# The down-projection's bias moved from the experts' loop to the tail of a mixture-of-experts kernel

## The reference, cut to what matters

```python
logits = (xt @ w_router).astype(jnp.float32) + b_router
top_vals, top_idx = lax.top_k(logits, TOP_K)
gates = jax.nn.softmax(top_vals, axis=-1)
...
def expert_block(args):              # 128 tokens of one expert
    gt = xb @ w_gate[e] + b_gate[e]
    up = xb @ w_up[e] + b_up[e]
    ...
    return hdn @ w_down[e] + b_down[e]
...
y = ybuf[dest] * sg[:, None]         # times the gate of (token, expert)
h = h + (the sum of y over a token's 4 experts)
gate = jax.nn.sigmoid(rms_norm_2(h, ple_gate_norm[i]) @ w_ple_gate[i])
e = rms_norm_2(p[i] @ w_ple_proj[i], ple_post_norm[i])
h = h + gate * e
```

## Time and profile before

| what | us |
|---|---|
| median of 3 runs | 2180.78 |
| lowest and highest run | 2180.38, 2182.97 |
| the profiled execution | 2176.34 |
| its span, first to last instruction | 2174.5 |
| TensorE busy | 2102.9 (97% of the span) |
| VectorE busy | 1533.1 (71%) |
| ScalarE busy | 1379.0 (63%) |
| GpSimd busy | 254.8 (12%) |

### The profile page before, as it was taken

One profiled execution on the slowest core, in us unless ns is written; L12 is line 12 of the kernel. 1 busy time (PEld: TensorE's weight loads), 2 busy tenths in 40 slices (PEclk: granted clock), 3 DMA queues, 4 the chain that ended last, 5 costly groups with the idle time before them and its releaser, 6 DMA issues.

```text
span 2174.5 us, 31913 instructions
## 1 busy us (share of the span) xinstructions
PE 2102.9 (97%) x10614; PEld 1733.1 (80%) x10614; DVE 1533.1 (71%) x1844; ACT 1379.0 (63%) x1838; POOL 254.8 (12%) x263
## 2 busy tenths in 40 slices
PE   7997899999999998979999999999999999999999
PEld 7886778888888886768888888888888888888877
DVE  4246744232333686688989898989898989898974
ACT  3146645222323444548888888888888888888873
POOL 0000000000000000012121212212121212121210
PEclk9998999999999999989999999999999999999999
DMA  5230112222233221369999999999999999999971
GB/s 185 74 134 27 52 49 88 97 97 87 92 112 119 89 96 39 122 232 361 370 370 359 366 367 356 370 361 366 358 372 359 375 362 366 358 373 355 371 277 43
DMA packets 86560, 511.27 MB, mean 235 GB/s; under 512 B 17285, under 2 KB 18905, under 8 KB 28890
## 3 DMA queue, kind: packets, MB, share of 16 engines
q1 hardware_dynamic: 71312, 487.61, 59.8%
q0 software_dynamic: 9536, 16.81, 3.1%
q10 hardware_dynamic: 5642, 5.91, 1.0%
HBM read 503.44 MB, written 23.07 MB: 242 GB/s over the span
## 4 chain that ended last, share of the span: by engine, by line
PE 90%; DVE 4%; ACT 2%; issue 2%; DMA 1%; ACTq 0%; POOL 0%; SPq 0%; POOLq 0%; DVEq 0%
PE PS L2544 16%; PE PS L2546 16%; PE PS L2545 16%; PE PS L256 10%; PE PS L257 10%; PE PS L258 10%; PE PS L2541 2%; PE PS L2440 1%; PE PS L2554 1%; PE PS L1156 1%; PE PS L1864 1%; PE PS L1085 1%; DVE AR L1127 1%; PE PS L1801 1%; PE PS L1794 0%
## 5 line engine op out<-in xcount | busy, mean ns | idle before, releaser
L2434 DVE TENSOR_TENSOR WL<-RING,WH 128x2048 fp32r<-128x2048 f32 x385 | 873.0, 2288 | 96.1 <-ACT WH L2414 93.0
L2414 ACT ACTIVATE WH<-RING 128x1024 fp32r<-128x1024 f32 x770 | 805.9, 1059 | 181.9 <-PE PS L2546 176.3
L2544 PE MATMUL PS<-WH,RA 128*128 128x512 f32 x1540 | 640.2, 416 | 0.0
L2546 PE MATMUL PS<-WH,RA 128*128 128x512 f32 x1540 | 601.5, 391 | 0.0
L2545 PE MATMUL PS<-WL,RA 128*128 128x512 f32 x1540 | 601.0, 390 | 0.0
L2546 PEld LDWEIGHTS PS<-WH,RA 128*128 128x128 f32 x1540 | 289.8, 188 | 63.0
L2545 PEld LDWEIGHTS PS<-WL,RA 128*128 128x128 f32 x1540 | 290.6, 189 | 59.1
L2544 PEld LDWEIGHTS PS<-WH,RA 128*128 128x128 f32 x1540 | 291.6, 189 | 54.6
L256 PE MATMUL PS<-WH,RA 128*128 128x512 f32 (+2 forms) x592 | 229.5, 388 | 7.1 <-POOLq L2735 3.6
L258 PE MATMUL PS<-WH,RA 128*128 128x512 f32 (+2 forms) x592 | 226.3, 382 | 0.0
L257 PE MATMUL PS<-WL,RA 128*128 128x512 f32 (+2 forms) x592 | 226.0, 382 | 0.0
(11 more groups left out here) (381 smaller groups left out, 2354.1 us busy)
## 6 DMA issues: line engine op xcount, KB each, us to landing
RING<-w_experts SPq DMA_DIRECT2D x390, 1024.0 KB, 7.2
RING<-w_front SPq DMA_DIRECT2D x60, 1024.0 KB, 4.9
X<-x SPq DMA_DIRECT2D x4, 512.0 KB, 5.8
acc_scr<-X SPq DMA_DIRECT2D x4, 512.0 KB, 4.7
xs_scr<-AR SPq DMA_DIRECT2D x4, 512.0 KB, 3.0
X<-acc_scr SPq DMA_DIRECT2D x4, 512.0 KB, 5.3
out<-X SPq DMA_DIRECT2D x8, 256.0 KB, 2.0
AR<-AR ACTq DMA_DIRECT2D x12, 128.0 KB, 2.4
```

The lines of the kernel that those rows point to most:

```text
L2414: e.activation(WH[:, m % 3, v], RING[:, m % 6, v], ACT.Copy).then_inc(s("m_hi"), 1)
L2434: e.tensor_tensor(WL[:, m % 3, :], RING[:, m % 6, :], WH[:, m % 3, :].bitcast(F32), ALU.subtract).then_inc(s("m_lo"), 1)
L2544: e.matmul(PS[bank][:, :], lhs[0][:, kr + k, :], WH[:, m % 3, c], start=False, stop=False)
L2546: x = e.matmul(PS[bank][:, :], lhs[1][:, kr + k, :], WH[:, m % 3, c], start=False, stop=(stop and k == 3))
```

## The change

- In the loop, pieces 8 and 9 start without the bias matmul, the first matmul of the piece with `start=True` instead. `SELD`, its copy on GpSimd and the semaphore `g_sed` are gone.
- Ahead of the loop, 16 matmuls transpose the one-hot matrix times gates (`OHG`, three bf16 parts) into 96 rows (part, expert) of 512 tokens; ScalarE copies them to `GDT`; three matmuls with `SEL3` repeat each part's 32 rows three times, and ScalarE copies them to `GDW`. ScalarE's copy to `GDT` stands ahead of its split of piece 3, the copies to `GDW` behind it, and TensorE waits for the last of them (`a_gd`) before it enters the loop. VectorE writes `IDB` (a bf16 identity) and `SEL3` in `dve_route_constants`.
- In the tail, 24 matmuls (8 outputs of 3) multiply `GDW` with the bias rows of `b_down`, and VectorE adds each output to `X` before `X` is transposed.
- The first four steps of the transposes of `X` run token block by token block instead of column block by column block, each block waiting for its sums (`v_xb`).
- The load of `PP` is issued by ScalarE at the end of `act_route`; its 8 transposes and their splits (`PPT`) stand ahead of the loop.

```diff
@@ pe_late_lists
+            e.wait_ge(s("v_ohg"), 1)
+            for i in range(4):
+                for k in range(4):
+                    x = e.matmul(PS[3][0:96, i * 128:(i + 1) * 128], OHGR[:, 4 * i + k, :], IDB, start=(k == 0), stop=(k == 3))
+            x.then_inc(s("p_gd"), 1)
             for i in range(4):
                 for k in range(4):
-                    if i == 0 and k == 0:
-                        e.wait_ge(s("v_ohg"), 1)
                     x = e.matmul(PS[4][:, 0:96], SLOT1[i][:, k, :], OHG[:, 4 * i + k, :, :], start=(i == 0 and k == 0), stop=(i == 3 and k == 3))
             x.then_inc(s("p_rt"), 1)
+            e.wait_ge(s("a_gd"), 1)
+            for w in range(3):
+                e.matmul(PS[1 + w][0:96, :], SEL3[0:96, w, :, :].rearrange("p j e -> p (j e)"), GDT, start=True, stop=True).then_inc(s("p_gd"), 1)
@@ act_route (end)
+            e.dma_start(PP, A["p_2"][0, 0].rearrange("(i p) c -> p i c", p=128)).then_inc(s("d_p"), 16)
@@ act_experts_start
+            for j in range(2):
+                e.wait_ge(s("p_xt"), XT["emb"] + j + 1)
+                e.activation(PPT[0][:, j, :], PS[6 + j][:, :], ACT.Copy).then_inc(s("a_xt"), 1)
...
+            e.wait_ge(s("d_xs"), 64)
+            e.wait_ge(s("p_gd"), 1)
+            e.activation(GDT, PS[3][0:96, :], ACT.Copy).then_inc(s("a_gd"), 1)
             act_expert_split(e, 3, 16, MM_LEAD + 1)
+            for w in range(3):
+                e.wait_ge(s("p_gd"), w + 2)
+                e.activation(GDW[:, w, :], PS[1 + w][0:96, :], ACT.Copy).then_inc(s("a_gd"), 1)
@@ pe_experts_start
+            e.wait_ge(s("d_p"), 16)
+            pe_split_T(e, "emb", PP, 2, (6, 7))
             e.wait_ge(s("d_xg"), 16)
...
             pe_late_lists(e)
+            e.wait_ge(s("a_gd"), 4)
@@ pe_expert
-            e.wait_ge(s("g_sed"), it + (b + 1))
...
-            pe_gemm(e, 8, 4, H2, SELD, 2048, 0, False)
+            pe_gemm(e, 8, 4, H2, None, 0, 0, False)
...
-            pe_gemm(e, 9, 5, H2, SELD, 2560, 0, False)
+            pe_gemm(e, 9, 5, H2, None, 0, 0, False)
@@ pool_expert
-            e.wait_ge(s("p_mm"), it * 24 + (b * 24 + 19 + MM_LEAD))
-            e.tensor_copy(SELD[0:96, 0:128], SELN[0:96, bass.ds(it + b + 1, 1)].broadcast_to([96, 128])).then_inc(s("g_sed"), 1)
@@ pe_tail
-            e.wait_ge(s("d_p"), 16)
-            pe_split_T(e, "emb", PP, 2, (6, 7))
...
+            for n in range(8):
+                i, half = n // 2, n % 2
+                if n >= 4:
+                    e.wait_ge(s("v_emb"), n + 1)
+                for w in range(3):
+                    x = e.matmul(PS[n][:, :], GDW[:, w, i * 128:i * 128 + 128], B3[0:96, 2048 + 512 * half:2560 + 512 * half],
+                                 start=(w == 0), stop=(w == 2))
+                x.then_inc(s("p_bd"), 1)
             for i in range(4):
-                e.wait_ge(s(f"d_x{i}"), 32)
-            for j in range(8):
-                if j >= 4:
-                    e.wait_ge(s("v_xt"), XT["gate"] + j - 3)
+                e.wait_ge(s("v_xb"), max(4, 2 * i + 2))
+                for j in range(4):
+                    x = e.transpose(PS[j][:, i * 128:(i + 1) * 128], X[:, i, j * 128:(j + 1) * 128], IDT)
+                    if i == 3:
+                        x.then_inc(s("p_xt"), 1)
@@ dve_tail
+            for n in range(8):
+                ...
+                e.wait_ge(s("p_bd"), n + 1)
+                e.tensor_tensor(v, v, PS[n][:, :], ALU.add).then_inc(s("v_xb"), 1)
```

More of the change, by code:

```diff
@@ L152, in program @@
         SELB = sb("SELB", [128, 128 + NBLK + 16], BF16)
-        SELD = sb("SELD", [128, 128], BF16)
         IDX = sb("IDX", [128, 8], I32)
@@ L1968, in program @@
         DIAG4 = cols(o, 4, 128); o_d4 = o; o += 512
+        IDB = ar(o, 64).bitcast(BF16); o += 64
+        SEL3 = ar(o, 144).bitcast(BF16).rearrange("p (w j e) -> p w j e", w=3, j=3); o += 144
         WR = RT[:, 0:256].rearrange("p (k e) -> p k e", k=8)
@@ L1995, in program @@
         OHG = ar(o_emb + 1024, 768).bitcast(BF16).rearrange("p (m v e) -> p m v e", m=16, v=3)
+        OHGR = ar(o_emb + 1024, 768).bitcast(BF16).rearrange("p (m n) -> p m n", m=16)
+        GDT = HT.rearrange("p a n -> p (a n)")[0:96, 0:256].bitcast(BF16)
+        GDW = XGT.rearrange("p a n -> p (a n)")[0:96, 0:768].bitcast(BF16).rearrange("p (w n) -> p w n", w=3)
         BLM = ar(o_emb + 1792, 640).bitcast(BF16).rearrange("p (i k v n) -> p i k v n", i=4, k=4, v=5)
@@ L2239, in dve_route_constants @@
             e.tensor_copy(SELB[0:96, 0:128], SELN[0:96, 0:1].broadcast_to([96, 128])).then_inc(s("v_selb"), 1)
-            e.tensor_copy(SELD[0:96, 0:128], SELN[0:96, 0:1].broadcast_to([96, 128])).then_inc(s("v_selb"), 1)
+            e.tensor_copy(IDB, IDT).then_inc(v_c.sem, v_c.up())
+            for w in range(3):
+                x = e.tensor_copy(SEL3[0:96, w, :, :], mid(IDT[0:96, 32 * w:32 * w + 32], 3))
+            x.then_inc(s("v_selb"), 1)
         def dve_route(e):
@@ L2404, in program @@
         LO_LEAD, MM_LEAD = 6, 24
+        PPT = tuple(RA[:, 6144 + 1024 * n:7168 + 1024 * n].rearrange("p (k n) -> p k n", k=2) for n in (0, 1))
         def act_expert_split(e, m, w_loaded, mm_done):
@@ L2491, in dve_experts_start @@
             dve_expert_split(e, 3, 8)
+            for j in range(2):
+                e.wait_ge(s("a_xt"), XT["emb"] + j + 1)
+                e.tensor_tensor(PPT[1][:, j, :], PS[6 + j][:, :], PPT[0][:, j, :].bitcast(F32), ALU.subtract).then_inc(s("v_xt"), 1)
         def pe_experts_start(e):
@@ L2543, in pe_gemm @@
                 c = slice(512 * k, 512 * k + 512)
-                e.matmul(PS[bank][:, :], lhs[0][:, kr + k, :], WH[:, m % 3, c], start=False, stop=False)
+                e.matmul(PS[bank][:, :], lhs[0][:, kr + k, :], WH[:, m % 3, c], start=(sel is None and kr == 0 and k == 0), stop=False)
                 e.matmul(PS[bank][:, :], lhs[0][:, kr + k, :], WL[:, m % 3, c], start=False, stop=False)
@@ L2780, in pe_tail @@
                 x.then_inc(s("p_t2"), 1)
-            for i in range(4):
-                e.wait_ge(s(f"d_x{i}"), 32)
-            for j in range(8):
-                if j >= 4:
-                    e.wait_ge(s("v_xt"), XT["gate"] + j - 3)
+            for n in range(8):
+                i, half = n // 2, n % 2
+                if n >= 4:
+                    e.wait_ge(s("v_emb"), n + 1)
+                for w in range(3):
+                    x = e.matmul(PS[n][:, :], GDW[:, w, i * 128:i * 128 + 128], B3[0:96, 2048 + 512 * half:2560 + 512 * half],
+                                 start=(w == 0), stop=(w == 2))
+                x.then_inc(s("p_bd"), 1)
+            for i in range(4):
+                e.wait_ge(s("v_xb"), max(4, 2 * i + 2))
[3 more added lines that the diff above has]
+                        x.then_inc(s("p_xt"), 1)
+            for j in range(4, 8):
+                e.wait_ge(s("v_xt"), XT["gate"] + j - 3)
                 for i in range(4):
@@ L2817, in act_tail @@
         def act_tail(e):
-            for j in range(2):
-                e.wait_ge(s("p_xt"), XT["emb"] + j + 1)
-                e.activation(PPT[0][:, j, :], PS[6 + j][:, :], ACT.Copy).then_inc(s("a_xt"), 1)
             for n in range(8):
@@ L2851, in dve_tail @@
         def dve_tail(e):
-            for j in range(2):
-                e.wait_ge(s("a_xt"), XT["emb"] + j + 1)
-                e.tensor_tensor(PPT[1][:, j, :], PS[6 + j][:, :], PPT[0][:, j, :].bitcast(F32), ALU.subtract).then_inc(s("v_xt"), 1)
             e.wait_ge(s("d_row"), 80)
@@ L2860, in dve_tail @@
                                 ).then_inc(s("v_emb"), 1)
+            for n in range(8):
+                i, half = n // 2, n % 2
+                v = X[:, i, 512 * half:512 * half + 512]
+                if half == 0:
+                    e.wait_ge(s(f"d_x{i}"), 32)
+                e.wait_ge(s("p_bd"), n + 1)
+                e.tensor_tensor(v, v, PS[n][:, :], ALU.add).then_inc(s("v_xb"), 1)
             for j in range(8):
```

9 lines of the change are left out of this document (1 added, 8 removed).

## The result

The changed kernel takes 2169.60 us (median of 5 runs, 2167.75 to 2171.30) beside 2180.38 of before (5 runs, 2179.97 to 2182.97): ratio 0.9948, interval 0.9933 to 0.9962, some 11 us faster. I had forecast 2174.2 with a range down to 2170.5: the sign was right, the gain too small. The profiled execution takes 2169.93, close to what I had forecast for it (2169.7), but two more profiled executions of the same kernel took 2173.88 and 2171.84: this agreement was partly chance.

The account below looks back on a forecast made before the run. TensorE's queue was taken to bound the kernel (90% of the chain). Loop -14.6, entry +1.7 and tail +6.3 made -6.6 us, from 2180.78 to 2174.2 us, range 2170.5 to 2179.0 (the forecast's own 2171 to 2176.8).

Parts of the forecast that it names:

- my sum: Whole kernel: loop -14.6, ahead of the loop +1.7, tail +6.3, in all -6.6 us.
- the loop's term: Experts' loop: 64 bias matmuls leave TensorE's queue at 0.22 to 0.23 us each, -14.6 us, not above 14.7.
- the base: Starting time the sum was taken from: the median of before, 2180.78 us, 4.44 above its profiled execution.
- The entry: Ahead of the loop: PP's early load and transposes 1.0 plus TensorE's wait for ScalarE's copies 0.7, +1.7 us.
- The load and transposes of `PP`: Ahead of the loop: tokens' transposes queue behind those of PP, 0.9 us later, plus 0.1 for loads sharing DMA engines.
- The wait for `a_gd`: Loop's start: TensorE waits for ScalarE's third copy to GDW until 954.7 against 954.06, losing 0.7 us.
- The tail: Behind the loop: 24 bias matmuls 5.5 us plus 0.8 for the transposes' new order, sums hidden, +6.3 us.
- the order: Tail: column block 0 is complete only with the 13th transpose, so the fifth step comes later, 0.8 us.
- TensorE's longer idle time ahead of the embedding's product: Start of the tail: TensorE idle a microsecond longer, the clock might lose or win about 1.7 us; taken as 0.
- Loads: Rival: DMA loads pace the loop, period stays 35.89 us, the loop gives nothing: 2188.8 us, chance 0.08.
- Entry and tail give back more: Rival: load and gather delay each other, copies and a sum come late: -2.6, 2178.2 us, chance 0.13.
- TensorE's 0.23 turns into a wait: Rival: in the loop, pieces 8 and 9 wait for hidden values or banks, half the gain goes: 2181.5 us, chance 0.06.

Follow-up runs that it names:

- e5: Kernel before without the loop's two bias matmuls a pass, copy to SELD and its wait kept, bias left out of the output: 2166.26 us, ratio 0.9926.
- e4: Kernel before with only the load, transposes and splits of PP moved ahead of the loop, biases staying in the loop: 2181.33 us, ratio 1.0005.
- e8: Changed kernel with the embedding's product started right behind the loop, not waiting for GpSimd's last count: 2166.18 us, ratio 0.9933 to before.
- e3: Changed kernel with load, transposes and splits of PP put back into the tail, so only the bias is moved: 2169.57 us, ratio 0.9947 to before.
- e1: Kernel before, unchanged, against itself: 2178.91 us (11 runs), ratio 0.9997.
- e9: Kernel before, unchanged, run again for a third trace: 2179.35 us, ratio 0.9993 to itself.
- e12: Kernel before with each of the loop's two bias matmuls of down issued twice in a row: 2192.35 us, ratio 1.0055.
- e6: Kernel before without the loop's bias matmuls, GpSimd's copy to SELD and the wait for it, bias left out of the output: 2163.64 us, ratio 0.9920.

## Why the prediction was wrong, step by step

The forecast of 2174.2 is 4.6 us above the measured 2169.60. The traces place 1.7 of that in my sum (-6.6, measured -8.3), 1.4 of it in the loop's term; 0.4 is the base, whose median was 2180.78 over three runs and 2180.38 over five; and 2.4 stand in none of the stretches that the edits touch. With the loop's term right the forecast would have been 2172.8, inside my range; it took the open 2.4 as well to bring the time below 2170.5.

**The step that failed: the loop's term, -14.6, measured -16.0.** The mechanism (the matmuls' place in TensorE's queue, nothing late behind them) held: period shorter, ScalarE still released by TensorE, no load in the way. But I priced a bias matmul by its one step in the chain, 0.22 or 0.23, and wrote that the cut could not be above 14.7. The removal gives 0.25 (e5), since the steps of its neighbours shrink too. That bound was no bound: the chain's rows show the step of the matmul, not how long its neighbours' steps are without it.

**The entry: +1.7, measured +1.6, and this nearness is luck.** The load and transposes of `PP`: 0.9 to 1.0, measured 0.86 in the first pair (940.43 to 942.74, less the 1.45 by which the exponential was later) and 1.0 in e4. The size held, the wait was another. I had the tokens' transposes queue behind those of `PP`, with 0.1 for the loads sharing the DMA engines; but in all seven traces with the early load TensorE is done with `PP` and idle for 0.16 to 0.30 us until the tokens' gather lands. The queue behind `PP` alone would have given some 0.2 less. From the gather's issue to the transposes it took 4.3 to 4.6 us with `PP` loaded late and takes 5.1 to 5.3 with `PP` loaded just ahead of it. The issue in before, which answers to 937.57 above:

```profile
936.11 1.22 POOL L2509 DMA_INDIRECT AR<-xs_scr,SMALL  x1 [5.19 <-DVE AR L2324]
```

The wait for `a_gd`, which I put at 0.7, did not bind in after's three traces: in the first, ScalarE is done at 953.94 and TensorE waits for VectorE until 954.15. It did bind, for 0.68, in e8's, where the lower clock reached to 952.5 and TensorE's late lists came later. The bias's own preparation costs 0.1 (e3). From the exponential to the loop's first matmul the whole is 0.66 (means of three). The other 0.94 come between that matmul and the first copy of `SELB`: 17.6 to 18.4 us in before, of which 2.0 to 3.4 are at the lower clock; 18.9 to 19.2 in after, with 4.7 to 5.3; and 16.7 in e8's trace, with none. Half of the 2.1 us by which the means of the lower clock differ is 1.05, so the clock is enough to account for it. This is the clock that I had weighed for the tail alone.

**The tail: +6.3, measured +6.1.** 24 x 0.216 = 5.2 in place of 5.5, the order 0.8 as forecast, and the sums were hidden. I had used the loop's price for the tail's matmuls. The Trainium skill, "TensorE: Matmul & The Clock Gate", section "Wait — 56ns, not 53.3ns?", has 216 ns for 512 columns; the bf16 row of matmuls in the tail agrees to the nanosecond, the loop's fp32r steps of 0.227 don't. For TensorE's longer idle time ahead of the embedding's product (4.95 us for 3.2 to 3.6) I had taken 0, and that held in the mean: the product took 13.00, 13.12 and 13.08 us in after and 12.62, 13.04 and 13.54 in before.

**The base: what is left of the 10.8.** The stretches behind the exponential give -8.3 (-16.0 + 1.6 + 6.1), and 2.4 us are left. Whole spans hide this: over three traces each they are 2176.7 and 2170.0 us in the mean, 6.6 apart, the number of my forecast, but only because the exponential starts 1.7 us later in after's, where no edit reaches. That agreement is luck too. The timed runs carry their granted clock: 0.9819 in the mean over 67 runs of before, 0.9830 over 15 of after. At two levels, 1.2 and 2.4 GHz, that is 2 x 0.0181 x 2178 = 79 us and 2 x 0.0170 x 2168 = 74 us at the lower one. Five us less of it, at half the speed, would be worth 2.5, the missing amount, but the runs don't bear that out. Among the 67 runs of before a time falls by 0.9 us for each 0.001 of clock, so the difference is worth 1.0 (an estimate); and at an equal clock the two kernels are still 10.0 us apart (0.983: 7 and 8 runs), 9.5 (0.984: 10 and 4) and 8.4 (0.982: 17 and 2). The traces don't show such a difference of clock either (after's three have more of the lower clock, not less). So about 1 us may be the clock's, and where the rest lies, and whether the change makes any of it, stays open; also the same code read 1.3 us lower when it was compared with itself (e1, e9). My forecast took the profile's sum from a median 4.44 us away and gave its own range no width for that.

**The rivals.** Loads (2188.8): no, 382 GB/s. Entry and tail give back more (2178.2): no, they gave back 7.7, where this needed 12.0. TensorE's 0.23 turns into a wait: no, TensorE is busy for 36.00 of 36.00 us in the loop.

## What to carry to other kernels

A step read in a chain prices an instruction only where its neighbours' steps stay as they are. Here one bf16 matmul among fp32r ones was worth more than its step of 0.22 to 0.23 when it went (0.25), and a second one beside it cost less (0.20); bounds for a removal have to allow for both. Cut each trace at points that the change doesn't touch before comparing spans: here 3 to 7 us of difference between executions lay ahead of the change. A sum that comes out right can hold a wrong wait: look at what ended each idle time, not at the size alone. And look for the engine that bounds the kernel standing idle behind a wait that covers more than the next step needs: moving that step ahead of the wait gave back 3.4 to 3.8 us here, more than half of the tail's 6.1 (e8).

## What the runs showed of the hardware

In the rows below, a copy on GpSimd that starts inside an operation of VectorE lasts until that operation ends. In before:

```profile
1517.20 4.48 DVE L2434 TENSOR_TENSOR WL<-RING,WH 128x2048 fp32r<-128x2048 f32 x2
...
1519.81 2.03 POOL L2700 COPY SELD<-SELB 96x128 bf16 x1 [2.77 <-PE PS L2546]
...
1521.80 0.18 POOL L2704 COPY SMALL<-SMALL 128x1 f32 x1
```

In the kernel without the bias matmuls (e5) the same copy of 96x128 came 0.18 us before the seam of VectorE's two splits and took 0.32, and the next one, of one column, took 2.23:

```profile
1516.96 4.58 DVE L2434 TENSOR_TENSOR WL<-RING,WH 128x2048 fp32r<-128x2048 f32 x2
...
1519.07 0.32 POOL L2700 COPY SELD<-SELB 96x128 bf16 x1 [2.27 <-PE PS L2546]
...
1519.35 2.23 POOL L2704 COPY SMALL<-SMALL 128x1 f32 x1
```

They end with the seam or the end of VectorE's splits (1519.24 and 1521.54), within 0.2 us. In e12 the copy of 96x128 came later in the split and took 1.63. The Trainium skill, "SBUF — State Buffer", section "🔬 SBUF: two separate sides", describes a port pair that the two share as an exclusive lock for a whole instruction when VectorE reads two inputs from SBUF; these rows agree (2.03 and 0.32 us for one copy). It cost this kernel nothing: no engine waited for the copy, and without it (e6) the stretches are no shorter.
